# Softmax probabilities of one attention branch turned by VectorE in 32x32 blocks, in place of TensorE and a copy out of PSUM

## The reference

```
logits = einsum('btgrd,btkgd->btgrk', qg, kg) * A_SCALE      # per head r of key head g
logits = where(valid, logits + bias, -inf)
p = softmax(logits, axis=-1)
o = einsum('btgrk,btkgd->btgrd', p, vg)
```

## The kernel before

| step | TensorE | ScalarE | VectorE |
|---|---|---|---|
| 0 | turns q (and k for r = 0) into PSUM, line 740 | copies them to QKT, line 1223 | |
| 1 | scores into bank 6, line 763 | exponentials SC to PR with sums, 1239 and 1240 | scales and adds the bias, two maxima, 1770 to 1777 |
| 2 | | | |
| 3 | turns the probabilities PR into bank 7, three 128x128 transposes, line 770 | copies bank 7 to PT, 128x384, line 1245 | |
| 4 | six value products PT by V into bank 4, line 792 | | 1 / sum, line 1786; gated rows OF, line 1796 |
| 5 | turns OF into bank 5, line 800 | high part to U, line 1254 | low part to U, line 1842 |

## Time and profile before

### The profile page before, as it was taken

How to read it: one execution, slowest core, us unless ns; L and a number is a source line. 1 busy time by engine, 2 the same in 40 slices (tenths; PEclk the granted TensorE clock), 3 DMA queues, 4 the chain that set the end, 5 groups by cost and what they waited for, 6 DMA issues and landing times.

```text
span 2411.3 us, 34025 instructions
## 1 busy us (share of the span) xinstructions
PE 2402.8 (100%) x10845; PEld 1983.9 (82%) x10845; DVE 1800.5 (75%) x2488; ACT 1237.5 (51%) x1597; POOL 322.1 (13%) x281
## 2 busy tenths in 40 slices
PE   9999999999999999999999999999999999999999
PEld 7888888878888888888888888888887888888887
DVE  5467679887888988888888897567767645587584
ACT  5445454555455444444444455455557555655443
POOL 0021242234210000000000000011101000521050
PEclk9999999999999999999999999999999999999999
DMA  8655555576655665555556556965554545555655
GB/s 270 193 188 179 174 178 175 188 246 219 226 185 185 202 196 192 192 192 194 186 192 199 193 190 214 248 189 177 179 183 161 180 161 177 180 166 167 227 189 167
DMA packets 134826, 464.24 MB, mean 193 GB/s; under 512 B 14544, under 2 KB 21328, under 8 KB 134112
## 3 DMA queue, kind: packets, MB, share of 16 engines
q1 hardware_dynamic: 122464, 443.08, 56.7%
q10 hardware_dynamic: 12256, 20.15, 2.8%
q0 software_dynamic: 32, 0.03, 0.0%
HBM read 455.87 MB, written 7.34 MB: 192 GB/s over the span
## 4 chain that ended last, share of the span: by engine, by line
PE 98%; DVE 1%; issue 0%; ACT 0%; ACTq 0%; DVEq 0%
PE PS L678 21%; PE PS L680 21%; PE PS L679 21%; PE PS L925 7%; PE PS L924 7%; PE PS L923 7%; PE PS L944 3%; PE PS L943 3%; PE PS L945 3%; PE PS L792 1%; PE PS L763 1%; DVE WL L1709 0%; PE PS L719 0%; PE PS L770 0%; PE PS L1096 0%
## 5 line engine op out<-in xcount | busy, mean ns | idle before, releaser
L1157 ACT ACTIVATE WH<-RAW 128x1024 fp32r<-128x1024 f32 x841 | 888.5, 1059 | 1078.7 <-PE PS L680 676.6
L1709 DVE TENSOR_TENSOR WL<-RAW,WH 128x1024 fp32r<-128x1024 f32 x811 | 1017.8, 1261 | 539.3 <-ACT WH L1157 529.1
L678 PE MATMUL PS<-WH,HT 128*128 128x512 f32 (+1 forms) x1816 | 717.3, 395 | 1.4 <-DVE HT L1741 1.2
L680 PE MATMUL PS<-WH,HT 128*128 128x512 f32 (+1 forms) x1816 | 706.3, 389 | 0.0
L679 PE MATMUL PS<-WL,HT 128*128 128x512 f32 (+1 forms) x1816 | 705.4, 388 | 0.0
L678 PEld LDWEIGHTS PS<-WH,HT 128*128 128x128 f32 x1816 | 341.1, 188 | 74.4 <-issue 5.2
L680 PEld LDWEIGHTS PS<-WH,HT 128*128 128x128 f32 x1816 | 340.8, 188 | 71.1
L679 PEld LDWEIGHTS PS<-WL,HT 128*128 128x128 f32 x1816 | 341.3, 188 | 67.5
L923 PE MATMUL PS<-WH,HT 128*128 128x512 f32 x704 | 274.0, 389 | 0.0
L925 PE MATMUL PS<-WH,HT 128*128 128x512 f32 x704 | 273.9, 389 | 0.0
L924 PE MATMUL PS<-WL,HT 128*128 128x512 f32 x704 | 273.9, 389 | 0.0
(11 more groups left out here) (317 smaller groups left out, 2306.7 us busy)
## 6 DMA issues: line engine op xcount, KB each, us to landing
RAW<-w_stream SPq DMA_DIRECT2D x841, 512.0 KB, 3.5
bias_scratch<-BE ACTq DMA_DIRECT2D x12, 256.0 KB, 3.2
MEMR<-mem_in ACTq DMA_DIRECT2D x1, 2048.0 KB, 10.6
X<-x_in ACTq DMA_DIRECT2D x4, 512.0 KB, 4.6
x_scratch<-X ACTq DMA_DIRECT2D x4, 512.0 KB, 4.9
X<-x_scratch ACTq DMA_DIRECT2D x1, 2048.0 KB, 11.5
out<-X ACTq DMA_DIRECT2D x8, 256.0 KB, 3.3
X<-x_in SPq DMA_DIRECT2D x3, 512.0 KB, 9.3
```

Source lines behind the costliest of these rows:

```text
L678: pe.matmul(o, hi, WH[:, slot, kk, 0:cols], start=k == 0, stop=False)
L680: ins = pe.matmul(o, lo, WH[:, slot, kk, 0:cols], start=False, stop=k == nq * GK - 1)
L1157: act.activation(WH[:, g.slot(j)], RAW[:, g.slot(j)], ACT.Copy).then_inc(hi_split, 1)
L1709: dve.tensor_tensor(WL[:, s], RAW[:, s], WH[:, s].bitcast(F32), ALU.subtract).then_inc(lo_split, 1)
```

## The change

For branch A alone, step 3 of TensorE and of ScalarE goes. VectorE gets a new function, `probs_turn`, which turns PR straight to PT, both in SBUF: 16 transposes of 32 partitions by 96 columns (three blocks of 32) a head. The source quarters 0 and 1 (8 instructions) stand in VectorE's step 2, the quarters 2 and 3 in its step 3, each behind the low split of that step and a wait for `probs`; the last of the 16 signals `pt_ready`, on which TensorE's step 4 waits as before. TensorE counts `pt_done` up behind the scores, so that the counts of later heads stay right.

```diff
+        TURNED_PROBS = [ASP, ]
...
                 ins.then_inc(scores, 1)
+                if any(br is b for b in TURNED_PROBS):
+                    pe.sem_inc(pt_done, 1)
...
             def a_step(i, p):
                 r = p // 6
-                st = head_steps(ASP, At(A0 + r, i, 4), lambda s: PAC[:, 2, s, ds(i * P + 256, P)], (0, 1, 3, 4, 5),
+                st = head_steps(ASP, At(A0 + r, i, 4), lambda s: PAC[:, 2, s, ds(i * P + 256, P)], (0, 1, None, 4, 5),
                                 1 if r else 2)
...
             def a_step(i, p):
                 r = p // 6
-                st = head_steps(ASP, At(A0 + r, i, 4), At(12 + r, i, 4), i * 4 + r, ("aq", "ak"), (0, 1, 3, 5), 1 if r else 2)
+                st = head_steps(ASP, At(A0 + r, i, 4), At(12 + r, i, 4), i * 4 + r, ("aq", "ak"), (0, 1, None, 5), 1 if r else 2)
...
+            def probs_turn(H, n, quarters):
+
+                dve.wait_ge(probs, H.count(1))
+                for a in quarters:
+                    for b in range(4):
+                        src = PR[32 * a:32 * a + 32, 0:n].rearrange("p (n s) -> p n s", s=P)[:, :, 32 * b:32 * b + 32]
+                        dst = PT[32 * b:32 * b + 32, 0:n].rearrange("p (n s) -> p n s", s=P)[:, :, 32 * a:32 * a + 32]
+                        ins = dve.transpose(dst, src)
+                if 3 in quarters:
+                    ins.then_inc(pt_ready, 1)
...
                 st = head_steps(ASP, At(A0 + r, i, 4), At(12 + r, i, 4), i * 4 + r, gate, (1, 4, 5))
                 if p - 6 * r in st:
                     st[p - 6 * r]()
+                elif p - 6 * r in (2, 3):
+                    probs_turn(At(A0 + r, i, 4), CAUS, (0, 1) if p - 6 * r == 2 else (2, 3))
```

## The result

The changed kernel takes 2465.34 us (median of 5 runs, 2464.09 to 2465.75) against 2412.99: a ratio of 1.0216, 95% interval 1.0206 to 1.0227, or 52.4 us more. The forecast was 2459.1 us, with a range of 2444 to 2464: the direction was right, the time 6.2 us more than forecast and 1.3 above the range.

What follows compares the result with a forecast made beforehand. TensorE, busy for all but 8.5 of 2411.3 us, was taken to bound the kernel. Late PT, 37.6 us, plus 8.4 for the clock gave 46.0 us on 2413.07: 2459.1 us, range 2444 to 2464.

Steps and rivals of the forecast that it cites:

- The lateness: Value products wait for PT behind VectorE's splits and transposes: 3.65 us at heads 0 and 2, 5.76 at 1 and 3.
- the step that a split and the transposes behind it don't overlap: In VectorE's queue, transposes start 1.26 us after the start of the low split ahead of them.
- the step on the clock: TensorE may run slower after waiting for PT: 0 to about 2.1 us more per long wait; 8.4 us charged.
- the four long waits: TensorE's waits for PT at heads 1 and 3, 6.5 us each, charged about 2.1 us each for the clock.
- the short waits: TensorE's four waits for PT at heads 0 and 2, 3.9 us each, charged nothing for the clock.
- rival 2: The waits at heads 0 and 2 lose the clock too, 8 x 2.1 us: 2467.5 us; chance 0.05.
- the other steps: Nothing else gets late behind PT; the 8 removed copies hasten nobody; TensorE's 0.33 us saved a head only lengthens its wait.
- Rival 4: VectorE's idle time hides the transposes; TensorE saves 2.6 us of transposes and 4 x 0.37 of waits: 2409.0 us; chance 0.03.

Runs made afterwards that it cites:

- run 1: Changed kernel plus unread 512-column matmuls ahead of TensorE's wait for PT, 14 at heads 0 and 2, 23 at heads 1 and 3: 2449.63 us.
- run 10: Changed kernel with scores and maxima, all 16 transposes, and reciprocal and gated rows each ahead of the low split of their step on VectorE: 2409.15 us.
- run 3: Changed kernel plus 23 unread matmuls ahead of TensorE's wait for PT at heads 1 and 3 alone: 2456.30 us.
- run 2: Changed kernel plus 14 unread matmuls ahead of TensorE's wait for PT at heads 0 and 2 alone: 2457.13 us.
- run 4: Changed kernel with 8 of the 16 transposes of a head, four in each step, half of PT not written: 2439.46 us.
- run 8: Changed kernel with all 16 transposes ahead of VectorE's low split of step 2, and scores and maxima ahead of that of step 1: 2410.71 us.
- run 9: Kernel before, without the change, with scaled scores and maxima ahead of VectorE's low split of step 1: 2412.57 us.
- run 5: Changed kernel without its 16 transposes; VectorE only signals PT, by a bare semaphore increment behind the low split of step 3: 2410.39 us.

## Why the prediction was right and wrong

**Right: that PT would be late, and why.** The order split, eight transposes, split, eight transposes stands in the trace as it was worked out. A transpose of 270 ns was predicted and 269 measured, eight in 2.26 us and 2.24 to 2.26. TensorE's weight loads were to wait 3.9 and 6.5 us, some 41 in all; they waited 4.0 to 4.1 and 6.4, and 41.7 in all (33.5 + 8.2 in the row of L796). The lateness was put at 37.6 us; run 1, with the clock at 1.00, has 36.6 us over the kernel before. The 1 us between comes from the step that a split and the transposes behind it don't overlap, 1.26 us from start to start: behind the first split of a pair the transposes start after 1.14 us (1942.27 to 1943.41), while that split lasts 1.23; eight times 0.12 us are 1.0.

The prediction weighed a figure of the Trainium skill (VectorE: DVE Perf Modes, The three transpose paths), 311 ns for a 128x128 of bf16. By it a head's turn was estimated at 0.93 us, less than a quarter of what it took: 16 instructions of 269 ns are 4.3 us a head, and the trace decides. That the Trainium skill leaves a 128x128 to TensorE (VectorE: DVE Perf Modes, Rules for kernel authors) fits what the change cost as it was placed, and not run 10.

**Wrong: the step on the clock.** "I charge the four long waits in full, as they are furthest from 1.1, and the four of 3.9 us not at all: 8.4 us." In place of 8.4 us the clock cost 15.7 (run 1). The larger part of the miss is the charge of nothing for the short waits. By the changed kernel's trace, where the clock's part is 16.0 us, they cost 1.4 to 1.6 us each (4.91 to 5.12 us from products to L804, against 3.53 with the clock at 1.00), 6.1 in all; in run 3's trace it is 6.0. The size for a long wait, 2.1 us, was near but low: behind them it was 2.1 to 2.8 us (5.59 to 6.32 against 3.53), 9.9 in all. That it was near is partly luck: it was the loss of the first nine matmuls of the kernel, no row tied that stretch to a wait in the stage, and in run 2 single long waits lost from 1.3 to 2.9. With the lateness 1.0 less and the clock 7.3 more than forecast, the 6.2 us are accounted for. The outcome is near rival 2, to which 0.05 was given and which gave 2467.5 us. It was argued away because 3.9 is little more than half of 6.5, and that is no reason: the trace of before had no wait between 1.1 us and this length, so it couldn't say whether 3.9 us is long enough for a fall. Run 4 shows a loss behind three of four waits of 3.67 us and none behind waits of 1.34 to 1.44; between these lengths nothing was run. The rule of the Trainium skill (TensorE: Matmul & The Clock Gate, Part 1) that the clock is halved after idleness agrees with the trace: 0.62 and 0.53 in the stretches behind the waits.

**Right as far as it went: the other steps.** Nothing else was late in the changed kernel: all that lies outside the two parts comes to -0.4 us. The copies that ScalarE and the transposes that TensorE no longer does bring nothing there, since both lie in front of a wait. Rival 4, faster through VectorE's idle time, needed "VectorE's order of work to be other than the trace shows"; with another order in runs 8 and 10 it is what happens, and run 10 has 2409.15 us where the rival had 2409.0. That the two are so close is luck, as errors of its sum cancel: at the four waits of L792 scores to products fell by 0.11 us each and not 0.37, the transposes were worth 0.37 a head and not 0.33, and the 3.53 us from products to L804 at heads 1 and 3, which the sum left alone, became 3.44.

## What to carry to other kernels

Work moved to an engine with idle time goes to the end of a queue: read its price from the place at which it stands and from what is due behind it, not from the engine's busy share. The same 128 transposes cost 52 us behind two splits that TensorE needed only two groups later, and saved 3.4 ahead of them, with the gated rows moved ahead too (run 10 against run 9); after such a move, look for the next line in the same queue, as L804 here. And where TensorE bounds the kernel and is made to wait, price its clock too: here each wait of 3.6 us or more was followed, with one exception in 20, by 1.3 to 2.9 us of loss.

## What the runs showed of the hardware

- TensorE's clock fell to the lower level (granted clock 0.53 and 0.62 in the mean of the stretches shown) behind waits of 3.6 to 5.9 us, and came back within the group behind the products. Behind a wait of 3.61 us the products still took 0.94 us and the slow starts came 1.6 us after TensorE had begun again (2050.99 to 2052.55). Behind waits of 3.67 us the clock held once in the profiled execution of run 4; behind 1.34 to 1.44 us it held at all four heads.
- Matmuls whose results nobody reads keep the clock up: 148 of them made the changed kernel 15.7 us faster, and the granted clock of the stage was 1.00 (run 1) instead of 0.90.
- A bare semaphore increment in VectorE's queue was seen by TensorE before the split ahead of it had ended: in run 5 the products of a head 3 begin at 1950.84, while the splits, the second of which stands ahead of the increment, run from 1949.81 to 1953.31.
- A wait of 0.37 us of a weight load between full groups cost 0.2 us of the stage by the trace (12.85 to 12.65 us from scores to the turn of OF, run 9), and 0.1 by the times (0.44 us for four).
- Eight transposes of 32x96 in fp32 lasted 2.24 to 2.26 us, 269 ns each in the mean; behind one split they started 1.14 us after its start, behind another 1.25 us.
